# A one-core transformer kernel on Trainium2: the steps of the first attention respaced with two bias buffers, and own PSUM banks for the outputs of the second attention

## The reference, cut to what matters

```python
# block 1, per layer
n = rms_norm(h, g_mix)
q, k, v, u, bg, cg, ga, gc = split(n @ w_in + b_in)
ya = chunked_rel_attention(q, k, v, g_q, g_k, rel_bias)  # 8 heads of 64, causal by chunks of 64, bias by distance
yc = bg * (conv_b + causal_conv3(cg * u, conv_w))
m  = sigmoid(ga) * (ya @ w_pa) + sigmoid(gc) * (yc @ w_pc)
h  = h + m @ w_o
h  = h + hier_moe(rms_norm(h))         # 32 experts, top 2 of one group
h  = h + sigmoid(rms_norm(h) @ w_ple_gate + b) * (p @ w_ple_proj)
# block 2: 16 meta tokens in front, two layers
#   layer 0: pool mixer, SwiGLU
#   layer 1: sliding_window_attention (16 query heads, 2 key heads, window 128, sinks, T5 bias), SwiGLU
```

## Time and profile before

| | us |
|---|---|
| median of 3 runs | 2139.97 (2133.69 to 2140.99) |
| the profiled execution | 2134.85 |
| its span in the profile | 2133.0 |
| TensorE busy | 1922.9 (90%) |
| VectorE busy | 978.3 (46%) |
| ScalarE busy | 650.1 (30%) |
| GpSimd busy | 181.3 (9%) |

### The profile page before, as it was taken

How to read it: one execution, slowest core, us unless ns; L and a number is a source line. 1 busy time by engine, 2 the same in 40 slices (tenths; PEclk the granted TensorE clock), 3 DMA queues, 4 the chain that set the end, 5 groups by cost and what they waited for, 6 DMA issues and landing times.

```text
span 2133.0 us, 33205 instructions
## 1 busy us (share of the span) xinstructions
PE 1922.9 (90%) x14316; PEld 1634.4 (77%) x14316; DVE 978.3 (46%) x1769; ACT 650.1 (30%) x1210; POOL 181.3 (9%) x170
## 2 busy tenths in 40 slices
PE   6887899949999989989799999997888969999997
PEld 4765788836666656668689999997765869999996
DVE  4744424352332233236974323357655574422456
ACT  5333323120110000126443222233555543222232
POOL 0012000000000000000300000013122330000012
PEclk9998999969999999999899999998999979999998
DMA  4211233548999999972202232243211224232242
GB/s 154 71 58 50 92 119 138 207 167 358 426 426 426 427 426 426 427 317 75 71 30 89 90 101 82 95 132 110 75 34 47 99 89 138 90 105 85 99 140 80
DMA packets 58087, 355.78 MB, mean 167 GB/s; under 512 B 6304, under 2 KB 8992, under 8 KB 45648
## 3 DMA queue, kind: packets, MB, share of 16 engines
q1 hardware_dynamic: 53968, 340.02, 41.5%
q0 software_dynamic: 3504, 12.73, 1.6%
q10 hardware_dynamic: 464, 0.85, 0.1%
HBM read 349.38 MB, written 4.19 MB: 166 GB/s over the span
## 4 chain that ended last, share of the span: by engine, by line
PE 69%; DVE 12%; DMA 10%; ACT 5%; issue 2%; POOL 2%; SPq 0%; DVEq 0%; ACTq 0%; POOLq 0%
PE bank L426 49%; DMA e<-in_we 9%; PE bank L611 7%; PE bank L633 4%; ACT SS L2451 1%; PE bank L472 1%; PE bank L644 1%; PE bank L760 1%; PE bank L645 1%; DVE scr L1272 1%; DVE wlo L1110 1%; DVE ztmp L1716 1%; DVE SS L1856 1%; DMA B<-in_rel 1%; DVE sm L1863 1%
## 5 line engine op out<-in xcount | busy, mean ns | idle before, releaser
L426 PE MATMUL bank<-nhi,whi 128*128 128x256 f32 (+2 forms) x1472 | 423.7, 288 | 3.5 <-DVE nlo L1726 1.9
L426 PE MATMUL bank<-nhi,wlo 128*128 128x256 f32 (+2 forms) x1472 | 419.5, 285 | 0.0
L426 PE MATMUL bank<-nlo,whi 128*128 128x256 f32 (+2 forms) x1472 | 419.4, 285 | 0.0
L1110 DVE TENSOR_TENSOR wlo<-raw,whi 128x1024 fp32r<-128x1024 f32 x243 | 303.4, 1255 | 139.8 <-ACT whi L1970 136.1
L1970 ACT CAST whi<-raw 128x1024 fp32r<-128x1024 f32 x247 | 256.9, 1042 | 127.1 <-PE bank L426 103.7
L426 PEld LDWEIGHTS bank<-nhi,whi 128*128 128x128 f32 x1472 | 279.4, 190 | 8.3 <-DVE nlo L1726 2.5
L426 PEld LDWEIGHTS bank<-nhi,wlo 128*128 128x128 f32 x1472 | 278.5, 189 | 1.4
L426 PEld LDWEIGHTS bank<-nlo,whi 128*128 128x128 f32 x1472 | 278.8, 189 | 0.9
L611 PE MATMUL bank<-e,xT 128*64 128x256 f32 x2048 | 236.1, 384 | 1.0 <-DVE xT L1401 1.0
L611 PEld LDWEIGHTS bank<-e,xT 128*64 128x64 f32 x2048 | 142.6, 137 | 82.3 <-issue 17.6
L426 PE MATMUL bank<-ghi,whi 128*128 128x256 f32 (+1 forms) x704 | 201.1, 286 | 0.0
(11 more groups left out here) (330 smaller groups left out, 2976.4 us busy)
## 6 DMA issues: line engine op xcount, KB each, us to landing
e<-in_we SPq DMA_DIRECT2D x96, 2048.0 KB, 36.0
raw<-in_w_down SPq DMA_DIRECT2D x64, 512.0 KB, 3.3
raw<-in_w_gate SPq DMA_DIRECT2D x48, 512.0 KB, 3.2
raw<-in_w_up SPq DMA_DIRECT2D x48, 512.0 KB, 3.3
raw<-in_w_q SPq DMA_DIRECT2D x12, 512.0 KB, 4.1
B<-in_rel POOLq DMA_DIRECT2D x8, 512.0 KB, 3.9
raw<-in_w_gc SPq DMA_DIRECT2D x8, 512.0 KB, 4.0
raw<-in_w_ga SPq DMA_DIRECT2D x8, 512.0 KB, 4.1
```

Source lines behind the costliest of these rows:

```text
L426: i = e.matmul(o, a, x[:, k0 + k, c0:c1], start=(k == 0 and n == 0), stop=(k == j.K - 1 and n == 2))
L1110: e.tensor_tensor(wlo[wslot(u)][:], raw[u % NRAW][:], whi[wslot(u)][:].bitcast(F32), ALU.subtract).then_inc(*hit("dve_low", ("lo", u)))
```

## The change

In the first attention each engine's generator is written as one loop in which the steps of a unit stand at even distances: on TensorE scores, two ticks, transposes of the unit before, two ticks, its PV product, two ticks. ScalarE copies the probabilities of the unit before ahead of the exponentials of this one. VectorE and ScalarE yield three times between their steps. The bias table has two buffers; table 1 is loaded at the very start, table 0 as before, table hp + 1 at t = 0 of hp = 1 and 2, its mask at t = 2. In the second attention the outputs take banks 2 and 3 in turn (`O2`) and no longer the side banks.

```diff
-    Bt = pl("B", [128, 2, S])
+    Bt = [pl("B0", [128, 2, S])]
...
+    Bt.append(pl("B1", [128, 2, S]))
...
         def pe_attention():
-            def second(un, hp, t):
-                (transposes of un)
-                yield
-                yield
-                (PV of un)
-            pend = None
-            for un in range(16):
-                (scores of un)
-                yield
-                if pend:
-                    yield from pend
-                if t == 0:
-                    take(("o1", hp), O2)
-                pend = second(un, hp, t)
-            yield from pend
+            for un in range(17):
+                if un < 16:
+                    (scores of un)
+                    yield from nothing(2)
+                if not un:
+                    continue
+                (transposes of pu = un - 1)
+                yield from nothing(2)
+                if t == 0:
+                    take(("o1", hp), O2)
+                (PV of pu)
+                yield from nothing(2)
...
-                    b = take(("o2", i - 2), SIDE)
+                    b = take(("o2", i - 2), O2)
...
         def dve_attention():
+            yield
+            for un in range(17):
+                if un < 16:
+                    (bias add and maximum of un)
+                    yield from nothing(3 if un else 2)
+                    w.wait_ge(*at("exp", un))
+                    e.reciprocal(st1[:, 2, c:c + 2], st1[:, 1, c:c + 2]).then_inc(*hit("dve_attn", ("rsum", un)))
+                if un:
+                    yield from nothing(3)
+                    (yalo of pu, if pu % 4 == 3)
...
         def act_attention():
+            for un in range(17):
+                yield from nothing(3)
+                if un:
+                    (copies of the turned probabilities of pu)
+                if un < 16:
+                    (exponentials of un)
+                if un:
+                    yield from nothing(3)
+                    (yahi of pu, if pu % 4 == 3)
...
         def pool_attention():
+            bias(1)
+            w.wait_ge(*at("turned x", 7))
+            bias(0)
+            mask(1)
+            mask(0)
             for un in range(16):
-                if t == 0:
-                    w.wait_ge(*(at("free", "sc", un - 1, 1) if un else at("turned x", 7)))
-                    (load of the bias of hp, and mask)
+                if t == 0 and 1 <= hp < 3:
+                    w.wait_ge(*at("free", "sc", un - 1, 1))
+                    bias(hp + 1)
+                if t == 2 and 1 <= hp < 3:
+                    mask(hp + 1)
```

More of the change, by code:

```diff
@@ L479, in pe_attention @@
         def pe_attention():
-            def second(un, hp, t):
-                n = (t + 1) * 128
-                X = Sc[un % 2]
+            for un in range(17):
+                if un < 16:
+                    hp, t = un // 4, un % 4
+                    n = (t + 1) * 128
+                    w.wait_ge(*at("qk", hp))
+                    w.wait_ge(*at("qk", 4 + hp))
+                    for x in range(2):
+                        b = take(("sc", un, x), SIDE)
+                        pb = 64 * x
+                        e.matmul(b[:, 0:n], qk[pb:pb + 64, hp, t * 128:(t + 1) * 128], qk[pb:pb + 64, 4 + hp, 0:n],
+                                 start=True, stop=True).then_inc(*hit("pe_attn", ("scores", un, x)))
+                    yield from nothing(2)
+                if not un:
+                    continue
+                pu = un - 1
+                hp, t = pu // 4, pu % 4
+                X = Sc[pu % 2]
                 for x in range(2):
-                    b = take(("pt", un, x), SIDE)
-                    w.wait_ge(*at("normed", un))
+                    b = take(("pt", pu, x), SIDE)
+                    w.wait_ge(*at("normed", pu))
                     for u in range(t + 1):
                         p = e.transpose(b[:, u * 128:(u + 1) * 128], X[:, x, u * 128:(u + 1) * 128], ident)
-                    p.then_inc(*hit("pe_attn", ("turned p", un, x)))
-                yield
-                yield
+                    p.then_inc(*hit("pe_attn", ("turned p", pu, x)))
+                yield from nothing(2)
+                if t == 0:
+                    take(("o1", hp), O2)
                 ob = bank[BANK["o1", hp]]
-                w.wait_ge(*at("PT", un))
+                w.wait_ge(*at("PT", pu))
                 w.wait_ge(*at("free", "v", hp // 2, 3))
@@ L498, in second @@
                                      PT[:, x, u, :], start=(u == 0), stop=(u == t))
-                p.then_inc(*hit("pe_attn", ("pv", un)))
-            pend = None
-            for un in range(16):
[L503 to L511, removed]
-                yield
-                if pend:
-                    yield from pend
-                if t == 0:
-                    take(("o1", hp), O2)
-                pend = second(un, hp, t)
-            yield from pend
+                p.then_inc(*hit("pe_attn", ("pv", pu)))
+                yield from nothing(2)
         def pe_conv():
@@ L690, in pe_turn_p, with nothing @@
                 p.then_inc(*hit("pe_turn", ("turned p2", c)))
+        def nothing(n):
+            for _ in range(n):
+                yield
         def pe_ple():
@@ L1163, in dve_attention @@
         def dve_attention():
[L1164 to L1193, removed]
@@ L1194, in dve_attention @@
-            yield from pend
+            yield
+            for un in range(17):
+                if un < 16:
+                    hp, t = un // 4, un % 4
+                    n = (t + 1) * 128
+                    X = Sc[un % 2]
+                    w.wait_ge(*at("B", hp))
+                    if un >= 2:
+                        w.wait_ge(*at("turned p", un - 2, 1))
+                    for x in range(2):
+                        w.wait_ge(*at("scores", un, x))
+                        e.scalar_tensor_tensor(X[:, x, 0:n], bk("sc", un, x, n=n), 0.125, Bt[hp % 2][:, x, 512 - n:512],
+                                               ALU.mult, ALU.add).then_inc(*hit("dve_attn", ("free", "sc", un, x)))
+                    c = 2 * un
+                    w.wait_ge(*last("dve_attn"))
+                    e.tensor_reduce(st1[:, 0, c:c + 2].unsqueeze(2), X[:, :, 0:n], AX.X, ALU.max, negate=True).then_inc(
+                        *hit("dve_attn", ("nmax", un)))
+                    yield from nothing(3 if un else 2)
+                    w.wait_ge(*at("exp", un))
+                    e.reciprocal(st1[:, 2, c:c + 2], st1[:, 1, c:c + 2]).then_inc(*hit("dve_attn", ("rsum", un)))
+                if un:
+                    pu = un - 1
+                    yield from nothing(3)
+                    if pu % 4 == 3:
+                        w.wait_ge(*at("ya hi", pu // 4))
+                        e.tensor_tensor(yalo[:, pu // 4, :], bk("o1", pu // 4), yahi[:, pu // 4, :].bitcast(F32),
+                                        ALU.subtract).then_inc(*hit("dve_out", ("ya", pu // 4), ("free", "o1", pu // 4)))
@@ L2049, in act_attention @@
-            yield from pend
+                    pu = un - 1
+                    n = (pu % 4 + 1) * 128
+                    if pu:
+                        w.wait_ge(*at("pv", pu - 1))
+                    for x in range(2):
+                        w.wait_ge(*at("turned p", pu, x))
+                        e.copy(PT[:, x, 0:pu % 4 + 1, :].rearrange("p a b -> p (a b)"), bk("pt", pu, x, n=n)).then_inc(
+                            *hit("act_attn", ("free", "pt", pu, x), *([("PT", pu)] if x else [])))
@@ new lines, in act_attention @@
+                if un < 16:
+                    n = (un % 4 + 1) * 128
+                    X = Sc[un % 2]
+                    c = 2 * un
+                    w.wait_ge(*at("nmax", un))
+                    for x in range(2):
+                        e.activation(X[:, x, 0:n], X[:, x, 0:n], ACT.Exp, bias=st1[:, 0, c + x:c + x + 1],
+                                     accum_out=st1[:, 1, c + x:c + x + 1]).then_inc(
+                                         *hit("act_attn", *([("exp", un)] if x else [])))
@@ L2051, in act_conv @@
+                if un:
+                    yield from nothing(3)
+                    if pu % 4 == 3:
+                        w.wait_ge(*at("pv", pu))
+                        e.copy(yahi[:, pu // 4, :], bk("o1", pu // 4)).then_inc(*hit("act_attn", ("ya hi", pu // 4)))
         def act_conv():
```

13 lines of the change are left out of this document (6 added, 7 removed).

## The result

The changed kernel takes 2106.78 us (median of 4, 2105.96 to 2107.5) against 2137.43 for the one before (4 runs): a ratio of 0.9856, 95% interval 0.9838 to 0.9874, or 30.7 us less. The profiled execution took 2106.93 us, its span is 2105.1; that is 27.9 us less than the profiled execution before.

The account below looks back on a forecast made before the run. TensorE was taken as the bound, with 69% of the chain. First attention 24.8 us, less 0.6 at the start, plus second attention 15.0, made 39.2 us off: 2101 us on the median's scale, range 2082 to 2122.

Parts of the forecast that it names:

- First attention: First attention with conv products: at most 41.9 us to gain, less 2.4, 11.7 and 3 for remaining costs, giving 24.8 us.
- The attention's own cost and the changes: First attention on TensorE: 31.5 us of attention work, plus 2.4 us for one extra dense-to-attention change per unit.
- The walk through the gate ends: First attention, conv tile ends at k steps 24, 48, 72, 96: PV waits of 1.9, 3.8, 1.6 and 3.6 us.
- The sign of being wrong that I had named: First attention: prediction wrong if the exponentials' order makes GpSimd late, so transposes wait for its multiplication; almost none before.
- Second attention: Second attention: outputs in banks 2 and 3 free the scores from waiting for nlo; 15.0 us gained, bounds 9 and 21.
- The ring: Second attention: VectorE's and ScalarE's loop per unit stays, 5.95 us a unit, and still outlasts TensorE's part.
- The start: Kernel start: bias 1 loaded beside x may delay the first x tile by up to 1.4 us; 0.6 taken.
- The port rule: First attention: GpSimd multiplications sharing VectorE's port could hold up all four conv outputs; gain 21.8 instead of 24.8 us.
- Slower by the clock: First attention: short, even waits hold TensorE at 1.2 GHz, up to 92 us more, 2189 us; chance 0.06.
- Second attention gives nothing: Second attention: VectorE's and ScalarE's ring was the bound, TensorE's waiting is only relabelled; 2116 us, chance 0.12.
- First attention keeps its ring: First attention: conv-end and copy waits at their upper bounds, gain falls to 11.5 us; 2114 us, chance 0.14.
- The waits at gate ends mostly vanish: First attention: ScalarE's copies come earlier and the clock stays up, part gives 36 us; 2089 us, chance 0.12.

Follow-up runs that it names:

- Moving the rounding away: Changed kernel with the rounding of all four conv outputs and its low part moved behind the next gate tile: 2089.6 us, ratio 0.9796.
- the old distances: First attention spaced 1, 2, 0 ticks, three a unit; kernel before with this spacing, two bias buffers and copies ahead of exponentials: 2117.91 us, ratio 0.9924.
- banks-only kernel: Kernel before with one edit, outputs of the second attention in banks 2 and 3: 2126.27 us, ratio 0.9953.
- late rounding: All four conv roundings moved later, with spacing 1, 2, 0 ticks, copies first, two bias buffers and own output banks: 2101.45 us, ratio 0.9837.

## Why the prediction came out as it did

The direction was right and 2106.8 lies in the range; the size was not: 39 us forecast, 30.7 measured (27.9 between the two profiled executions, 29.2 when both kernels ran again on one chip). The mechanisms held. The costs that stay in the first attention were taken too low, the gain of the second attention too high, and one loss was not in the sum.

- **First attention, 24.8 us forecast, 19.7 measured.** The stretch to k step 110 took 126.93 us where my sum gave 123.2 (106.1, 2.4, 11.7 and 3). *The attention's own cost and the changes* were mis-sized: 31.5 and 2.4, 33.9 together, against some 38. At full clock the trace after has, from the first matmul of a block to the next dense one, 0.43 to 1.06 us for scores, 0.14 to 0.82 for transposes and 0.37 to 1.03 for PV: some 31 us for the 16 units. On top of that the dense matmul ahead of scores or PV has a start gap of 0.31 to 0.33 us, and the one behind each of the three kinds 0.31 to 0.34, where between dense ones it is 0.23: 0.5 us a unit, some 7 to 8 us. I had counted one such change a unit and taken the others as inside the blocks. *Clock*: the spells at 1.2 GHz behind the two long waits stretched 3.2 us of work to 5.6 and 2.2 to 3.7, so 3.9 us, and I had taken 3. *Waits*: 9.3 us by TensorE's rows against 11.7. These sum to 126 us and leave about 1 open.
- **The walk through the gate ends held for three of four.** Forecast 1.9, 3.8, 1.6 and 3.6 us; measured 0.48 (0.4 more ahead of the weight load), 3.54, 1.08 and 3.02. The third showed on the transposes, behind GpSimd, and not on PV. Moving the rounding away took the waits from 9.3 to 2.8 us and the clock from 0.96 to 1.00, 11.0 us in all: the mechanism is shown.
- **What the parts are worth** I had not worked out. I had put the 26.8 us of copy waits down to the order, rightly, and counted on the spreading over 55 more k steps for the rest. The runs show copies ahead of exponentials (12.1 us alone) and two bias buffers (7.1 alone) giving 18.8 of the 19.7 us in the old distances. The even distances took away waits for GpSimd (10.1 to 1.9) and gave nearly all of it back: two more gate ends with waits of 1.1 and 3.0 us, and more changes. They are worth 9.5 us once the rounding is out of the way. With them the second bias buffer is worth 0.2. The sign of being wrong that I had named, transposes waiting for GpSimd, came mainly in the old distances (10.1 us) and hardly in the changed kernel (1.9).
- **Second attention, 15.0 forecast, 12.9 measured**, 12.8 with that edit alone. No score waits for `nlo` any more (15.4 us before). By group 2.5, 4.7, 4.0 and 1.1 (and 0.6 ahead of the first bias add) against 1.8, 5.0, 5.0 and 3.2. The ring was right, 5.85 us against 5.95. Groups 2 and 3 fell short at their first units: the second bias add followed the first by 5.84 and 6.05 us, not 4.7, with waits of 1.21 and 1.42 for scores. Those stand behind PV and transposes, which took 1.83 instead of 1.02 for PV at 1605.9, the 1.2 GHz level again. I had also said that the tables' loads remain on the path; loading them earlier changed nothing. At group starts the scores wait for the query tile, 6.3 us in 4 times, and that is as late as the table.
- **The start.** 0.6 us forecast, none measured: the first x tile lands after 4.27 us as before. What landed later had no effect: the x tiles at a median of 7.2 us and not 6.2, the row constants at 9.4 and not 8.0.
- **Passing through.** Nothing of a shift is lost up to the logits, nor between the experts and the second attention. In the experts' stage 4.0 us went, and my sum had nothing for that: the load that ends the stage came 1.5 us later against TensorE, and the clock fell behind the wait. The banks-only kernel, with the code of before up to there, shows the same loss, so no edit is needed for it; whether the change has a part in it stays open.
- **The port rule.** GpSimd's multiplication met the taps at the first end (3.05 us for the two) and at the third (2.62), and not at the second and fourth (1.54 each). VectorE's taps and the multiplications that they met, first end and then third:

```profile
138.21 3.05 DVE L1210 SCALAR_TENSOR_TENSOR yb<-zb,vec,yb 128x512 f32<-128x512 f32 x2
137.79 2.13 POOL L2573 TENSOR_TENSOR Sc<-Sc,st 128x1024 f32<-128x1024 f32 x1 [6.41 <-DVE st L1181]
...
194.58 2.62 DVE L1210 SCALAR_TENSOR_TENSOR yb<-zb,vec,yb 128x512 f32<-128x512 f32 x2
194.16 1.71 POOL L2573 TENSOR_TENSOR Sc<-Sc,st 128x768 f32<-128x768 f32 x1 [5.91 <-DVE st L1181]
```

The taps lose 1.5 us behind the longer multiplication and 1.1 behind the shorter, 0.2 less than was left of each when the taps came. The Trainium skill, SBUF — State Buffer, section SBUF: two separate sides, says that of a VectorE instruction with two SBUF inputs and a GpSimd one that reads SBUF the one that starts second blocks fully until the other is done; the trace agrees. The fear that all four would collide did not come true.

- **The rivals.** Slower by the clock: it rose from 0.89 to 0.96. Second attention gives nothing: refuted by the edit alone. First attention keeps its ring: only its gate ends do. The waits at gate ends mostly vanish: not here (8.1 us at the four); they did once the rounding was moved, and that kernel took the 2089.6 us that this rival had as its price.

## What to carry to other kernels

When an in-order engine serves two steps of a pipeline, put ahead the one whose consumer is nearer; in this kernel that one exchange was worth more (12.1 us alone) than the buffer (7.1) and the distances (0.9). Widening the distances exposes the pipeline to more of the main stream's own chains, so look for what every engine does at those places (here a rounding that nobody needed yet) before judging the distances. Parts that give little alone (on the old distances with copies first, even distances 0.9, late rounding 2.4) gave 11.9 us together, so test them in pairs. And for a part worth a microsecond or two measure from a mark just ahead of the stage: here a difference of 1.2 us became 0.2 and one of 0.3 became 2.4 once that was done.

## What the runs showed of the hardware

- TensorE's waits of 3.54 and 3.02 us in the changed kernel were followed by some 5 and 3.4 us at 1.2 GHz, and the wait of 2.64 us of the kernel before by some 3 (from 200.29). Waits of 0.4 to 1.25 us were not, nor was one of 2.20 at 158.60 with buffers and copies first. Behind the last load of the experts a wait of 3.3 to 3.6 us was followed by slow down products (8.43 to 10.06 us for 64, not 7.13) in nine profiles of ten.
- With all waits of TensorE under 1.3 us the granted clock was 1.00 over 116 us, in a stage whose matmuls come from four kinds of work.
- A change from dense matmuls to scores or PV, and back from any of the three kinds of attention work, showed as a start gap of 0.31 to 0.34 us where two dense matmuls have 0.23.
- The experts' stage, which ends on a load, took 517.0 to 522.1 us in thirteen profiles; a study of a few microseconds ahead of it should read marks, not only the total.
